# A two-block transformer kernel on one core: the order of ScalarE's waits in the downward projections, and small moves between engines in four stages

## What is computed

```python
# first block, for each of 2 layers
h = h + token_mixers(rms_norm(h, g_mix_norm[i]), ...)       # two attentions, gated
h = h + conv_ffn(rms_norm(h, g_ffn_norm[i]), ...)           # up, width-3 conv, gelu gate, down (2816 -> 1024)
h = h + sigmoid-gated projection of p[i]                    # "ple"
# second block, for each of 2 layers
n = rms_norm(x, g_mix[l]); ua, ub, uc, ud = split(n @ w_in[l])
y_a = conformer_conv(ua); y_b = hgrn2_bidir(ub)             # silu(layer_norm(...)); norm(o) * silu(g)
y_c = short_gated_conv(uc); y_d = mla(ud)                   # latent attention, 4 heads
cat = rms_norm of each of the 4 groups of [y_a, y_b, y_c, y_d]
x = x + cat @ w_out[l]
x = x + cross attention of rms_norm(x) over rms_norm(mem)   # mem: 256 rows
x = x + (silu(a1) * a3) @ f_w2[l]                           # a1, a3 = rms_norm(x) @ f_w13[l]
```

## Time and profile before

| | us |
|---|---|
| median of 3 runs | 3338.15 (3331.66 to 3342.27) |
| the profiled execution | 3342.28 |
| its span, first to last instruction | 3340.5 |
| mean granted clock of TensorE | 0.968 |

### The profile page before, as it was taken

How to read it: one execution, slowest core, us unless ns; L and a number is a source line. 1 busy time by engine, 2 the same in 40 slices (tenths; PEclk the granted TensorE clock), 3 DMA queues, 4 the chain that set the end, 5 groups by cost and what they waited for, 6 DMA issues and landing times. The chain is left out here.

```text
span 3340.5 us, 39165 instructions
## 1 busy us (share of the span) xinstructions
PE 3148.0 (94%) x14620; PEld 2460.0 (74%) x14620; DVE 1601.2 (48%) x2502; ACT 1457.9 (44%) x2313; POOL 1582.6 (47%) x870
## 2 busy tenths in 40 slices
PE   8999999999999999999999978899999887989999
PEld 6666788878866578887877746678877763758887
DVE  2773357721367435773249644433214953443320
ACT  5836543333484654333343574532223257352321
POOL 4634555545564455554465342344444533334444
PEclk8999999999899999999999988999999997999999
DMA  3221233333222123233332101133333200223333
GB/s 117 64 64 50 82 99 97 95 101 99 74 70 64 45 76 101 95 99 100 101 96 76 39 20 57 57 101 95 95 95 98 69 24 32 63 64 97 97 102 102
DMA packets 73741, 265.09 MB, mean 79 GB/s; under 512 B 8657, under 2 KB 9169, under 8 KB 73169
## 3 DMA queue, kind: packets, MB, share of 16 engines
q1 hardware_dynamic: 73552, 262.59, 25.6%
HBM read 260.46 MB, written 2.10 MB: 79 GB/s over the span
## 5 line engine op out<-in xcount | busy, mean ns | idle before, releaser
L365 POOL TENSOR_TENSOR low<-raw,high 128x1024 fp32r<-128x1024 f32 x482 | 1175.1, 2440 | 1260.1 <-ACT high L356 1228.2
L380 PE MATMUL bank<-slot_r,low 128*128 128x512 f32 (+2 forms) x3636 | 1430.1, 393 | 0.0
L381 PE MATMUL bank<-slot_r,high 128*128 128x512 f32 (+2 forms) x3636 | 1428.0, 393 | 0.0
L379 PE MATMUL bank<-slot_r,high 128*128 128x512 f32 (+1 forms) x3316 | 1329.4, 401 | 58.4 <-POOL low L365 19.1
L356 ACT ACTIVATE high<-raw 128x1024 fp32r<-128x1024 f32 x482 | 506.8, 1054 | 839.7 <-PE bank L381 744.9
L379 PEld LDWEIGHTS bank<-slot_r,high 128*128 128x128 f32 x3316 | 632.3, 191 | 235.1 <-issue 59.2
L381 PEld LDWEIGHTS bank<-slot_r,high 128*128 128x128 f32 (+1 forms) x3636 | 692.9, 191 | 149.2
L380 PEld LDWEIGHTS bank<-slot_r,low 128*128 128x128 f32 (+1 forms) x3636 | 693.9, 191 | 147.6 <-issue 8.2
L1598 DVE SCALAR_TENSOR_TENSOR tmp<-padded,small,tmp 128x512 f32<-128x512 f32 x176 | 209.9, 1251 | 0.0
L866 POOL TENSOR_SCALAR tmp<-tmp,stat 128x512 f32<-128x512 f32 (+3 forms) x128 | 75.4, 589 | 170.0 <-DVE stat L840 147.4
L2081 DVE SCALAR_TENSOR_TENSOR slots<-padded,small,slots 128x512 f32<-128x512 f32 x128 | 135.2, 1114 | 0.0
(11 more groups left out here) (318 smaller groups left out, 3463.3 us busy)
## 6 DMA issues: line engine op xcount, KB each, us to landing
raw<-w SPq DMA_DIRECT2D x482, 512.0 KB, 3.6
slots<-x_in SPq DMA_DIRECT2D x4, 512.0 KB, 6.5
slots<-mem_in SPq DMA_DIRECT2D x2, 1024.0 KB, 4.9
out<-slots SPq DMA_DIRECT2D x8, 256.0 KB, 4.8
const<-const_in SPq DMA_DIRECT2D x1, 1073.5 KB, 10.3
padded<-p_in SPq DMA_DIRECT2D x2, 512.0 KB, 5.7
tmp<-masks_in SPq DMA_DIRECT2D x1, 512.0 KB, 11.2
small<-small SPq DMA_DIRECT2D x2, 231.5 KB, 3.0
```

Source lines behind the costliest of these rows:

```text
L365: pool.tensor_tensor(self.low[:, t % PARTS, :], self.raw[:, t % RING, :], self.high[:, t % PARTS, :].bitcast(F32), ALU.subtract).then_inc( ...
L379: pe.matmul(acc, lhs[0], rhs[1], start=first, stop=False)
L380: pe.matmul(acc, lhs[1], rhs[0], start=False, stop=False)
L381: return pe.matmul(acc, lhs[0], rhs[0], start=False, stop=last)
```

## The change

- In the downward loops of `first_tail` and `second_tail` ScalarE waits for exactly the tiles that finish chunk c (`down_done`), and splits one tile further before it waits for `x_down`.
- In `second_mixer` the two Silus of G move from before the latent copies to after head 2.
- In `second_attention` the high half of `mem` is made by VectorE instead of ScalarE (`high_dve`), its low half moves to the end of the step, and VectorE waits for the load of `mem` at step 3. After branch A's Silus ScalarE squares the four slices of branches A and B.
- In `second_tail` ScalarE squares only the other four slices, the first two group sums wait for nothing, and TensorE's wait for `value_ready` moves from before the cross attention to after the scores of its fifth and sixth units.

```diff
@@ -507,6 +507,9 @@
 
     def high(self, act, c):
         act.activation(self.pairs[c][0], self.xs[c], ACT.Copy, scale=self.gain[c]).then_inc(self.sig("high"), 1)
+
+    def high_dve(self, dve, c):
+        dve.tensor_scalar(self.pairs[c][0], self.xs[c], self.gain[c], None, ALU.mult).then_inc(self.sig("high"), 1)
 
     def square(self, act, c):
         if c > len(self.squares):
@@ -1523,9 +1526,10 @@
                 hidden_high(FC - 2)
                 hidden_high(FC - 1)
                 for c in range(KC):
-                    for n in range(3):
-                        weights.split_high(act, ffn + 2 * FC + 3 * c + n + 3)
-                        act.wait_ge(sem("tile_done"), ffn + 2 * FC + 3 * c + n + 1)
+                    for t in range(down_done(c - 1) if c else 0, down_done(c)):
+                        weights.split_high(act, ffn + 2 * FC + t + 3)
+                        act.wait_ge(sem("tile_done"), ffn + 2 * FC + t + 1)
+                    weights.split_high(act, ffn + 2 * FC + down_done(c) + 3)
                     act.wait_ge(sem("x_down"), c + 1)
                     u3.high(act, c)
                     u3.square(act, c)
@@ -1991,9 +1995,6 @@
                     act.activation(S[:, LATENT_R[i], :], banks[i][:, :], ACT.Sqrt, scale=1.0 / features, bias=eps).then_inc(sem("latent_root"), 1)
                 for c in range(1, 4):
                     off_copies(c)
-                for c in range(2):
-                    act.wait_ge(sem("evacuated"), N - 1 + c)
-                    act.activation(S[:, G + c, :], S[:, G + c, :], ACT.Silu).then_inc(sem("silu_g"), 1)
                 for i, slot in enumerate((CQ, CQ + 1, CKV)):
                     act.wait_ge(sem("latent_out"), i + 1)
                     act.activation(LATENT[i][0], S[:, slot, :], ACT.Copy).then_inc(sem("latent_high"), 1)
@@ -2028,6 +2029,10 @@
                         for c in range(2):
                             act.wait_ge(sem("both"), c + 1)
                             act.activation(PT[:, 0, c, :], S[:, Y + 2 + c, :], ACT.Square).then_inc(sem("b_square"), 1)
+                    if j == 2:
+                        for c in range(2):
+                            act.wait_ge(sem("evacuated"), N - 1 + c)
+                            act.activation(S[:, G + c, :], S[:, G + c, :], ACT.Silu).then_inc(sem("silu_g"), 1)
                     if j == 4:
                         act.wait_ge(sem("head_sum"), 4)
                         act.wait_ge(sem("eps_ready"), 1)
@@ -2286,7 +2291,6 @@
             if step == 2:
                 act.wait_ge(sem("load_mem"), 16)
             if 2 <= step < 2 + KC:
-                memory.high(act, step - 2)
                 memory.square(act, step - 2)
             if step in (10, 12, 14):
                 weights.split_high(act, base + step // 2 - 4)
@@ -2294,6 +2298,10 @@
                 for c in range(2):
                     act.wait_ge(sem("standard"), c + 1)
                     act.activation(S[:, Y + c, :], S[:, TAP_A + c, :], ACT.Silu, scale=s2("ln_g", c), bias=s2("ln_b", c)).then_inc(sem("branch_a"), 1)
+                act.wait_ge(sem("branch_a"), 2)
+                act.wait_ge(sem("branch_b"), 2)
+                for n in range(4):
+                    act.activation(tmp[:, n, :], S[:, Y + n, :], ACT.Square).then_inc(sem("early_square"), 1)
 
         def side_dve(dve, step, place):
             if place == "end" and step in (3, 4):
@@ -2305,10 +2313,14 @@
                 c = step - 5
                 y = S[:, Y + 2 + c, :]
                 dve.scalar_tensor_tensor(y, y, s2("onorm", c), S[:, B_R + c, :], ALU.mult, ALU.mult).then_inc(sem("b_normed"), 1)
+            if place == "scores" and step == 3:
+                dve.wait_ge(sem("load_mem"), 16)
             if place == "scores" and 3 <= step < 3 + KC:
-                memory.low(dve, step - 3)
+                memory.high_dve(dve, step - 3)
                 if step >= 4:
                     memory.add(dve, step - 3)
+            if place == "end" and 3 <= step < 3 + KC:
+                memory.low(dve, step - 3)
 
         def side_pool(pool, n):
             if n in (8, 10):
@@ -2342,6 +2354,8 @@
         E64_MEM = PT[:, 0, 2, 0:MEM]
         K_SQ, K_R = PT[:, 0, 0, :], PT[:, 0, 1, :]
         def side_pe(pe, step, place):
+            if step == 4 and place == "scores":
+                pe.wait_ge(sem("value_ready"), 2)
             if step == 4 * NT + 4 and place == "turns":
                 out_tile.append(weights.next(pe))
                 pe.wait_ge(sem("o_low"), 1)
@@ -2387,7 +2401,8 @@
             @block.tensor
             def _(pe):
                 def group_sum(g):
-                    pe.wait_ge(sem("cat_square"), 2 * g + 2)
+                    if g >= 2:
+                        pe.wait_ge(sem("cat_square"), 2 * g - 2)
                     for b in range(NT):
                         for c in range(2):
                             mm = pe.matmul(banks[7 - g][:, b:b + 1], tmp[:, 2 * g + c, b * P:b * P + P], cst("ones")[:, 0:1], start=(c == 0), stop=(c == 1))
@@ -2466,7 +2481,6 @@
                     pe.matmul(banks[2 + c][:, :], cst("heads"), tmp[:, c, :], start=True, stop=True).then_inc(sem("query_sum"), 1)
                 value_half(1)
                 pe.wait_ge(sem("query_ready"), 2)
-                pe.wait_ge(sem("value_ready"), 2)
                 run_pe(pe)
                 for half in range(2):
                     w = out_tile[0] if half == 0 else weights.next(pe)
@@ -2492,7 +2506,7 @@
 
             @block.scalar
             def _(act):
-                for n in range(KC):
+                for n in range(4, KC):
                     act.activation(tmp[:, n, :], S[:, Y + n, :], ACT.Square).then_inc(sem("cat_square"), 1)
 
                 def cat_high(n):
@@ -2568,9 +2582,10 @@
                 weights.split_high(act, ffn + 2 * FC + 2)
                 hidden_high(FC - 1)
                 for c in range(KC):
-                    for n in range(3):
-                        weights.split_high(act, down_at + 3 * c + n + 3)
-                        act.wait_ge(sem("tile_done"), down_at + 3 * c + n + 1)
+                    for t in range(down_done(c - 1) if c else 0, down_done(c)):
+                        weights.split_high(act, down_at + t + 3)
+                        act.wait_ge(sem("tile_done"), down_at + t + 1)
+                    weights.split_high(act, min(down_at + down_done(c) + 3, end + 3))
                     if lead is not None:
                         act.wait_ge(sem("x_down"), c + 1)
                         lead.high(act, c)
```

## The result

The changed kernel takes 3307.54 us (median of 4 runs, 3306.20 to 3310.83), against 3340.21 us for the kernel before beside it (3331.66 to 3342.30): ratio 0.9908, 95% interval 0.9889 to 0.9928, so 24 to 37 us less. The profiled execution took 3310.83 us (span 3309.0) against 3342.28 (span 3340.5), that is 31.45 us less where the prediction's sum had 32.3.

A forecast was written before the change was run, and what follows sets the result against it. TensorE is busy for 94% of the span, so time comes off only where it waits or runs at the lower clock afterwards. -25.6 - 4.8 + 2.0 - 2.4 - 1.5 = -32.3 us: from 3338.15 to 3306 us, range 3296 to 3318.

The forecast's parts named there:

- Part 1: Downward loops: ScalarE's new order of waits and splits removes the stall in three of four loops, gaining 25.6 us.
- rival (e): Downward loops: ScalarE still meets x_down before the sixth tile is split, only the other changes count: 3331.5 us; chance 0.04.
- rival (b): First block's two tails: stall moves to a late eighth or ninth raw tile, 4 us back each, 3314 us; chance 0.05.
- Part 2: Second mixer: Silus of G behind head 2 start the latent copies 2.43 us earlier; gain 4.8 us, between 3.5 and 6.5.
- the stage shifts as a whole: Second mixer: the chain behind the latent copies starts from them on VectorE too, so all moves earlier, 2.4 us a layer.
- Part 3: Latent attention: memory's high half on VectorE costs +1.0 us a layer, +2.0 in all.
- Rival (d): Latent attention: GpSimd blocks VectorE's 32 halves, 2.07 us each, up to 3372 us, decisive from 16 on; chance 0.02.
- Part 4: Tail's opening: four squares moved into the latent attention let column sums start earlier; gain 1.2 us a layer, 2.4 in all.
- What is late next is TensorE's own work: Tail's opening: without the squares' wait, TensorE's column sums set the pace, so 1.2 us a layer is gained.
- Rival (c): Tail stage: TensorE's shorter idle keeps the upper clock, some 4 us more a layer, 3298 us; chance 0.08.
- Part 5: Cross attention: with the value_ready wait moved, scores start 0.75 us earlier; gain 1.5 us in two layers, between 0 and 2.
- Rival (a): Whole kernel: only the downward loops' gain counts, smaller gains are eaten or another engine ends last, 3312.6 us; chance 0.09.

The follow-up runs named there:

- e1: Kernel before with only the new order of ScalarE's waits and splits in the downward loops of both tails: 3316.76 us, 21.7 less.
- e5: Kernel before with only memory's high half moved from ScalarE to VectorE in the latent attention: 3338.34 us, 0.3 more.
- e6: Kernel before with only the four squares of branches A and B moved to step 19 of the latent attention: 3340.49 us, 2.0 more.
- e2: Changed kernel with the downward loops' new order of waits and splits undone, all else kept: 3331.88 us, 6.0 less than the kernel before.
- e10: Changed kernel keeping only the downward loops' new order and the moved Silus of G: 3309.66 us, 27.7 less than the kernel before.
- e12: Kernel before with only the gated layers' fourth tile split ahead of the two norm instructions in the second block's tail: 3336.36 us, 2.3 less.
- e7: Kernel before with only the wait for value_ready moved behind the first scores of the cross attention: 3339.55 us, 2.0 more.
- e3: Kernel before with only the two Silus of G moved behind head 2 in the mixer: 3336.55 us, 2.7 less.
- e9: Changed kernel run again unaltered, as a control: 3309.29 us, 28.7 less than the kernel before.
- e11: Changed kernel with the gated layers' fourth tile split ahead of the two norm instructions in the second block's tail: 3312.09 us, 26.7 less than the kernel before.
- e8: Kernel before with 12 matmuls of constants filling TensorE's idle ahead of the latent projection in the mixer: 3343.04 us, 2.3 more.

## Why the prediction came out as it did

**Part 1, right but for 1.5 us.** 25.6 was forecast; the stages give 24.1 and the time of e1 21.7 (17.0 to 26.4). All three loops shrank to the pattern of the fourth, and the extra split ahead cost nothing, as costed. The adds 4.16 us apart exclude rival (e), and the 92 us without idle behind them rival (b), a stall at the eighth or ninth tile. What the sum had no term for is the unchanged code behind the first loop, where 1.5 us went to the clock.

**Part 2, the mechanism right, its size off.** The idle fell by 2.47 us, and behind head 2 the Silus held nobody. In the stage the part is worth 3.0 to 4.0 us a layer on average instead of 2.4, and 4.3 and 4.8 in the changed kernel; the two layers together pass the range of 3.5 to 6.5. The step that failed is "the stage shifts as a whole": the projection behind a shorter idle also runs at a higher clock, save where it was at 1.00 already. In the time the part shows 2.7 us (5.7 to -0.3).

**Part 3, right in its steps.** +1.0 a layer was forecast, +0.8 measured on VectorE; four steps of 9.6, 9.58 measured. What follows in the stage moved by more than that, either way (-1.3 us in both stages of e5, +2.1 and +0.1 in the changed kernel), and the time shows none of it (e5). Rival (d) is out: one instruction a layer was blocked, by 0.83 us, and not 16.

**Part 4, wrong.** 1.2 us a layer was forecast, 0.05 and 0.27 arrive in e6. The freed time is even larger where it arises, 2.07 us. The step that failed is "What is late next is TensorE's own work": it was priced at the clock that it had before, and followed for one step and not to the end of the stage. In the changed kernel the sums started 1.2 us earlier, ran at 0.50 throughout, and TensorE came to the memory's sum 6.84 us behind the opening instead of 6.52. Rival (c) let the clock only give at this place; the sums took 4.33 us for 5.46 in e6 and 6.95 in the changed kernel, but kernels without the part have 5.46 and 6.99 as well, and no tail ended 4 us earlier.

**Part 5, wrong in the same way.** The 0.75 us is there (0.84), grows to 1.9, and 0.17 to 0.23 arrive. The copies did not become the bound, and the moved wait never held, as reasoned. The step that failed is that what the scores gain reaches the end: I had looked for a rival engine, and not for the next stall, 60 us on, where a gain of this size costs 1.7 us of clock.

**So the total is right with errors that cancel.** In the profiled execution parts 4 and 5 lack 3.9 us, part 1 lacks 1.5, part 2 has 4.3 more, and the start 0.5. Rival (a), that only part 1 counts, is excluded for parts 2 to 5 together by e2 (3.3 to 9.0 less); for parts 3 to 5 it fits what happened with part 1 in place (e10).

**Open.** What decides whether the stretch behind a stall gets the upper or the lower level. The runs show that it differs where nothing in the code does (e1, e5 and e12 have the second mixer 3.1 to 3.7 us shorter without touching it), that the one kernel profiled twice repeats its pattern, and that at one stall it goes with the stall's place in the stage (e7). Why, no run shows. Nor is it settled why parts 3 to 5 gain 4.7 us without part 1 (e2 against e3) and 0.4 with it (e10 against e9). Whether TensorE would keep part 5's gain without the stall was not settled, as e11 put another one there.

## What to carry to other kernels

Price a stall by its idle and by the clock behind it, and add up only gains that are followed to the end of their stage. One of 1 to 2 us that meets a further stall of TensorE can be taken back there, as both were here. Gains of 8 us, as from the order of ScalarE's waits and splits, are well above this. Before a step is moved into an engine's idle time, look at the engine that takes up its output: here GpSimd's half of the split slowed VectorE by 2 us.

## What the runs showed of the hardware that I had not expected

The granted clock behind a given stall is not a price to look up. The same 2.6 us of idle was followed by 5 us at 1.00 in the kernel before and at 0.66 in e7, after a shift of 1.9 us, and over 24 tails the level went with the time at which this stall ended (e7); the runs of e8 fall in two groups some 10 us apart. The Trainium skill (TensorE: Matmul & The Clock Gate, What's actually happening) states that the activity window is free-running and does not begin anew with the kernel. That would fit the spread between the runs, which is not shown; it does not explain by itself that two profiled executions of one kernel agree within 0.1 us in seven stages, though one came to them 2.5 us later than the other.

Filling an idle with 2.9 us of matmuls of constants raised the clock of the next 10 us from 0.83 to 1.00, and no gain from it can be measured in the time.
